# Wider products for up tiles 52 to 95 of an expert layer, and every fourth late tile's rest made by an adding DMA

## Chip, cores and metric

The kernel runs on one core of one Trainium2 chip. The metric is the device time of one launch in microseconds (us), the median of the runs shown; lower is better.

## What is computed

The reference is a stack of four blocks on 256 tokens of width 1024, in float32. The change touches only the expert layer ("PEER"), which stands in the first stack twice. Cut to what matters, and written as this kernel does it:

```
q      = h @ w_q                        8 heads, two halves of 128
scores = q_half @ sub_keys.T            top 16 of each half, then top 16 of the pairs
g      = softmax(top scores)            16 of 16384 experts, per head and token
up     = h @ peer_u.T                   256 x 16384: all experts, 128 tiles of 128
act    = gelu(up) * (sum of g at the chosen experts, else 0)
y      = act @ peer_v                   16384 x 1024: 128 down tiles
x      = x + gate * y
```

The kernel computes every expert for every token and weights the result, instead of gathering the chosen ones.

## The kernel before

Weights stream from HBM as tiles of 128 x 1024 float32 (512 KB) into a ring of four slots (`ring`, `RING = 4`). `refill` in the SyncE block issues the load of tile n+4 once tile n's slot is free, which is when `split_ready` counts tile n. All refills go through SyncE's one queue, in the order of `SEGMENTS`; beside them, at the start of `up0_late` and `up1_late` (the refill that tile 56 releases), SyncE runs `gate_row_out_sp`, which writes one row of 1024 values to HBM as 4-byte pieces (L784).

Products are float32 in three passes: each operand is split into a rounded high part and a rest, and high x high, high x rest and rest x high are summed. For the weights ACT makes the high part (`high`, L266, a rounding copy) and the DVE or POOL the rest (`rest`, L275, tile minus high), into one of four places of `wsplit`. `high(n)` waits for the tile and for PE to be done with tile n-4.

An up tile j gives 128 experts for all 256 tokens: eight chunks of the contraction. A narrow tile (`lin_cols`, `passes`, L240) takes three products of 256 columns per chunk, 24 in all. A wide tile (`wide_passes`, L246 and L247) takes two: the high part of the weights against the input's high part and rest side by side (512 columns, whole PSUM bank), and the rest against the high part (256 columns into the first half). Its two halves have to be added afterwards: ACT copies the second half out (L1567), the DVE adds the first (`summed`, L1706), and only then ACT takes the Gelu (L1570). Before the change tiles 30 to 50 are wide.

From tile 52 on the late phase runs: a routing step of four tokens stands behind seven of every eight tiles (`STEP_AT`, 64 steps). For step q the DVE builds one-hot matrices (`onehots`, L1741, `weighted_onehots`, L1747), PE multiplies them (`routing`, L1489), the DVE weights the tiles done so far for those tokens (`weigh`, L1714 and L1715), and ACT keeps the factors of later tiles in the places of their activations (`keep`, L1594). For a tile j in this phase the first `kept` tokens' Gelu stays in PSUM (L1574), the others go to the activations (L1576), and the DVE multiplies the kept ones by their factors (`weigh_tile`, L1723).

PE waits at the start of `up(j)` for `activated_ready` and `pr_weighted` of tile j-3, since three PSUM banks turn. The orders of ACT and DVE are written out by hand: ACT runs `keep` of tile j-1, `activate(j)` and in it `high` of tile j+3; the DVE's loop turn j runs the steps' work, the rest of tile j+2, the sum of tile j and the weighing of tile j-1. An instruction that waits holds everything behind it on its engine.

```python
for j in range(HEAD, 129):
    if j + 1 in STEP_AT: onehots(with_step(j + 1))
    if j - 1 in STEP_AT: weigh(with_step(j - 1))
    if j + 1 in STEP_AT: weighted_onehots(with_step(j + 1))
    if j + 2 < 131: up_rest(j + 2)
    if j < 128 and wide(j): summed(j)
    if j - 1 >= FIRST_STEP: weigh_tile(j - 1)
```

## Time and profile before

| | us |
|---|---|
| median of 3 runs | 2568.08 (2567.43 to 2568.27) |
| the profiled execution | 2567.51 |
| its span, first to last instruction | 2565.6 |
| PE busy | 2512.6 (98%) |
| DVE busy | 2037.3 (79%) |
| ACT busy | 1415.9 (55%) |
| POOL busy | 321.9 (13%) |
| granted TensorE clock | 0.994 of full speed |

The rows further down come from this one execution. Times are counted from its first instruction. A busy PE means that some product was in flight; the duration of one product contains its way through the array, so the pitch from one tile's start to the next is what a tile costs. "Idle before" names what ended an engine's wait.

### The profile page before, as it was taken

The page shows a single profiled execution, that of the slowest core. Times are in us where ns is not written, and L with a number is a line of the kernel's source. Part 1 is how long each engine was busy: PE and PEld are TensorE (multiplying, and loading weights), DVE is VectorE, ACT ScalarE, POOL GpSimd, SP SyncE. Part 2 cuts the span into 40 slices and gives each one's busy share as a digit, 9 for nine tenths or more (in the row PEclk, how much of TensorE's full clock was granted, in tenths as well). Part 3 has the DMA queues.
Part 4 walks back from the last instruction along what each step waited for, and adds up shares of the span by engine and source line. Part 5 has one row for each costly group of instructions (what it writes and reads, how often), then busy time and mean ns, then how long its engine had stood idle before and what let it go on. Part 6 is the DMA issues. An engine that isn't in the chain of part 4 may idle for free.

```text
span 2565.6 us, 46053 instructions
## 1 busy us (share of the span) xinstructions
PE 2512.6 (98%) x16116; PEld 2249.3 (88%) x16116; DVE 2037.3 (79%) x3624; ACT 1415.9 (55%) x2303; POOL 321.9 (13%) x182
## 2 busy tenths in 40 slices
PE   6999999999999999999999999999999999999998
PEld 5779989999888888889989999888888888889887
DVE  6778978899888887679888898666666886688766
ACT  3455575544565666555675545665554554464553
POOL 3107800000000002627500000000000001000000
PEclk9999999999999999999999999999999999999999
DMA  6844575444888885434664445555555355543554
GB/s 227 289 161 167 184 251 165 160 161 159 283 289 286 292 282 161 156 103 169 203 227 161 161 157 179 193 194 200 193 194 190 117 180 193 192 167 113 193 184 140
DMA packets 138422, 492.37 MB, mean 192 GB/s; under 512 B 18705, under 2 KB 18793, under 8 KB 137985
## 3 DMA queue, kind: packets, MB, share of 16 engines
q1 hardware_dynamic: 135600, 481.90, 55.3%
q0 software_dynamic: 2640, 8.02, 0.9%
q8 instruction: 118, 1.93, 0.3%
q14 instruction: 64, 0.52, 0.1%
HBM read 488.79 MB, written 1.07 MB: 191 GB/s over the span
## 4 chain that ended last, share of the span: by engine, by line
PE 87%; DVE 6%; DMA 3%; ACT 2%; issue 1%; POOL 0%; DVEq 0%; SPq 0%; ACTq 0%; POOLq 0%
PE ps L240 70%; PE ps L246 7%; PE ps L247 4%; PE ps L1489 2%; DMA weight_ring<-in_stream 2%; DVE weight_split L275 1%; ACT weight_split L266 1%; PE ps L2659 1%; PE ps L1453 1%; DVE hT_split L500 1%; DVE arena L742 0%; DVE hT_split L499 0%; DVE stat L625 0%; POOL weight_split L275 0%; PE ps L454 0%
## 5 line engine op out<-in xcount | busy, mean ns | idle before, releaser
L266 ACT ACTIVATE weight_split<-weight_ring 128x1024 fp32r<-128x1024 f32 x800 | 849.5, 1063 | 271.5 <-DMA weight_ring<-in_stream 181.6
L275 DVE TENSOR_TENSOR weight_split<-weight_ring,weight_split 128x1024 fp32r<-128x1024 f32 x684 | 830.4, 1222 | 163.7 <-ACT weight_split L266 161.6
L240 PE MATMUL ps<-hT_split,weight_split 128*128 128x256 f32 x7224 | 922.1, 286 | 3.9 <-POOL weight_split L275 1.5
L240 PE MATMUL ps<-weight_split,hidden_split 128*128 128x512 f32 x3948 | 911.6, 390 | 0.1
L240 PEld LDWEIGHTS ps<-hT_split,weight_split 128*128 128x128 f32 x7224 | 884.3, 192 | 10.3 <-issue 6.9
L240 PEld LDWEIGHTS ps<-weight_split,hidden_split 128*128 128x128 f32 x3948 | 735.9, 188 | 156.7 <-issue 1.4
L275 POOL TENSOR_TENSOR weight_split<-weight_ring,weight_split 128x1024 fp32r<-128x1024 f32 x116 | 282.7, 2443 | 122.2 <-ACT weight_split L266 122.0
L246 PE MATMUL ps<-hT_split,weight_split 128*128 128x512 f32 x816 | 291.4, 398 | 0.5 <-DVE hT_split L500 0.5
L1584 ACT ACTIVATE hidden_split<-arena 128x256 fp32r<-128x256 f32 (+1 forms) x256 | 173.9, 679 | 148.1 <-PE ps L240 148.0
L247 PE MATMUL ps<-hT_split,weight_split 128*128 128x256 f32 x816 | 229.0, 281 | 0.0
L1758 DVE TENSOR_TENSOR hidden_split<-arena,hidden_split 128x256 fp32r<-128x256 f32 x256 | 163.6, 639 | 81.6 <-ACT hidden_split L1584 81.6
L246 PEld LDWEIGHTS ps<-hT_split,weight_split 128*128 128x128 f32 x816 | 153.3, 188 | 37.5 <-DVE hT_split L500 1.1
L240 PE MATMUL ps<-weight_split,hT_split 128*128 128x512 f32 x660 | 158.7, 397 | 3.1 <-DVE weight_split L275 2.6
L247 PEld LDWEIGHTS ps<-hT_split,weight_split 128*128 128x128 f32 x816 | 154.0, 189 | 2.6
L1574 ACT ACTIVATE ps<-ps 128x256 f32<-128x256 f32 (+45 forms) x152 | 40.9, 269 | 208.0 <-PE ps L240 208.0
L240 PEld LDWEIGHTS ps<-weight_split,hT_split 128*128 128x128 f32 x660 | 123.7, 190 | 30.3 <-DVE weight_split L275 3.6
L1576 ACT ACTIVATE arena<-ps 128x256 f32<-128x256 f32 (+36 forms) x206 | 99.4, 483 | 75.5 <-PE ps L240 75.5
L742 DVE CUSTOM_DVE_ANT_0 arena<-weight_ring,silu_c_row 128x1024 f32<-128x1024 f32 x104 | 126.7, 1219 | 6.5 <-DMA weight_ring<-in_stream 5.5
L937 DVE TENSOR_TENSOR arena<-arena,ps 128x256 f32<-128x256 f32 x62 | 26.1, 421 | 106.7 <-ACT arena L897 106.7
L1741 DVE TENSOR_TENSOR step_places<-arena 128x1024 f16<-128x1024 f16 x128 | 88.3, 690 | 16.4 <-PE ps L1489 15.2
L1747 DVE TENSOR_TENSOR arena<-step_places,pick_parts 128x1024 f16<-128x1024 f16 x128 | 88.0, 688 | 0.7
L1832 POOL DMA_DIRECT2D arena<-in_sb_pairs x1 | 0.6, 644 | 677.8 <-DVE arena L556 677.8
(377 smaller groups left out, 1924.6 us busy)
## 6 DMA issues: line engine op xcount, KB each, us to landing
weight_ring<-in_stream SPq DMA_DIRECT2D x912, 512.0 KB, 4.2
arena<-gate_rows SPq DMA_DIRECT2D x3, 512.0 KB, 5.2
x<-in_x SPq DMA_DIRECT2D x1, 1024.0 KB, 5.1
arena<-mlstm_m_rows POOLq DMA_DIRECT2D x1, 1024.0 KB, 6.1
arena<-in_ln_mix_g POOLq DMA_DIRECT2D x2, 512.0 KB, 5.3
arena<-in_ln_mix_b POOLq DMA_DIRECT2D x2, 512.0 KB, 7.5
arena<-in_ln_ffn_g POOLq DMA_DIRECT2D x2, 512.0 KB, 4.6
arena<-in_ln_ffn_b POOLq DMA_DIRECT2D x2, 512.0 KB, 6.5
```

The costliest lines, as they stand in the source:

```text
L240: mm = pe.matmul(out_, stationary(s_part), moving(m_part), start=start and n == 0, stop=stop and n == 2, skip_group_check=True)
L246: pe.matmul(ps[:, bank, :].rearrange("p (k t) -> p k t", k=2), stationary(HIGH), moving, start=start, stop=stop, skip_group_check=True)
L247: return pe.matmul(ps[:, bank, 0:T], stationary(REST), moving[:, HIGH, :], start=False, stop=stop, skip_group_check=True)
L266: act.activation(wsplit[:, n % SPLITS, HIGH, :], ring[:, slot(POS[n]), :], ACT.Copy).then_inc(high_ready, 1)
L275: eng.tensor_tensor(w[:, REST, :], ring[:, slot(POS[n]), :], w[:, HIGH, :].bitcast(fp32), ALU.subtract).then_inc(split_ready, 1)
L742: dve.tensor_tensor_reduce(products, ring[:, slot(ADA_POS[a]), :], silu_row[:], 1.0, 0.0, ALU.mult, ALU.add, dots[:, row % 2, c:c + 1]).th ...
L1489: mm = pe.matmul(ps[:, q % 3, 128 * a:128 * a + 128], step_places[:, q % 2, 0, a, :], step_weights_in[:, q % 2, part, a, :], start=part == ...
L1576: step = act.activation(acts(j)[:, kept:T], bank[:, kept:T], ACT.Gelu)
L1584: act.activation(hidden[:, j % 3, HIGH, :], acts(j, i), ACT.Copy).then_inc(hidden_high, 1)
L1741: dve.tensor_tensor(step_places[:, q % 2].rearrange("p n a (j d) -> p (n a) j d", d=2), two_iotas, pr_places[:, q].rearrange("p n a d -> p ...
L1747: step = dve.tensor_tensor(step_weights_in[:, q % 2].rearrange("p k a (j d) -> p k a j d", d=2), step_places[:, q % 2, 1].rearrange("p a ( ...
L1758: dve.tensor_tensor(hidden[:, j % 3, REST, :], acts(j, i), hidden[:, j % 3, HIGH, :].bitcast(fp32), ALU.subtract).then_inc(hidden_ready, 1)
```

## The change

`WIDE` adds tiles 52 to 95 to the wide ones. In these the second half goes to a contiguous place, `second_halves`, and the sum goes back into PSUM, so that the Gelu has its two targets as in a narrow tile. The DVE's turn is reordered: the sum of tile j-1 and the weighing of tile j-2 stand in turn j.

`added(j)` is true for tiles 56, 60, ..., 124, 18 in a layer. For these ACT writes the negated, rounded tile into the rest's place right after the high part of tile j-1, POOL issues a DMA that adds the tile from the ring to it (512 KB, SBUF to SBUF), and the DVE, instead of making the rest, waits for that DMA in the turn of tile j-1 and counts the tile as split by a one-column memset. The high part of such a tile is made at once after the Gelu of tile j-4.

Besides, the `iota` table of 128 x 128 no longer has a place of its own: POOL loads it with the expert layer's parameters and the DVE casts it after the top-16 search; the first waits for constants are for 16 instead of 32; `EDGE` grows by 64 words, `step_weights_in` moves behind `second_halves`, and `halves_before` is `2 * len(WIDE)`. Cut of these lines, the diff is:

```diff
...
 FIRST_STEP = STEP_AT[0]
 EARLY = 51
 EXP_AT = 14
+WIDE = [j for j in range(128) if 30 <= j < 51 or 52 <= j < 96]
 def slot(pos):
...
         STEP = 4
         STEPS = T // STEP
         assert len(STEP_AT) == STEPS and EARLY < FIRST_STEP
-        step_weights_in = edge_b.bitcast(fp16).rearrange("p (r k a j) -> p r k a j", r=2, k=2, a=STEP)
+        second_halves = arena[:, ROUTE + 64 + 2 * T:ROUTE + 64 + 3 * T]
+        step_weights_in = arena[:, ROUTE + 64 + 3 * T:EDGE].bitcast(fp16).rearrange("p (r k a j) -> p r k a j", r=2, k=2, a=STEP)
         (pr_par, pr_q_out, pr_scored, pr_s_out, pr_topped, pr_chosen, pr_exp_in, pr_exp, pr_cols_t, pr_cols_out,
          pr_places_r, pr_parts_r, pr_built, pr_routed, pr_kept, pr_weighted) = (sem("peer_" + s) for s in (
              "params_in", "q_out", "scored", "scores_out", "topped", "chosen", "exp_in_ready", "exp_ready", "cols_turned", "cols_out",
...
         def weighted_count(l, j):
             return (128 - FIRST_STEP) * l + j - FIRST_STEP + 1
+        def added(j):
+            return FIRST_STEP + 4 <= j < 125 and j % 4 == 0
+
+        def added_count(l, j):
+            return sum(added(m) for m in range(128)) * l + sum(added(m) for m in range(j + 1))
+
         def wide(j):
-            return 30 <= j < 51
+            return j in WIDE
         def wide_count(l, j):
             return sum(wide(m) for m in range(128)) * l + sum(wide(m) for m in range(j + 1))
...
         def peer_pool(l):
             pool.wait_ge(src_ready, src_done(4 if l else 1))
             pool.dma_start(pr_sk, io["sub_keys"][l]).then_inc(pr_par, 16)
-            pool.dma_start(pr_iota16, io["iota"][:, 0:16]).then_inc(pr_par, 16)
+            pool.dma_start(pr_iota32, io["iota"]).then_inc(pr_par, 16)
             rests_pool(FIRST[f"peer{l}q"] + 3, 13)
             rests_pool(FIRST[f"up{l}"], HEAD)
+            for j in range(128):
+                if added(j):
+                    n, k = FIRST[f"up{l}"] + j, added_count(l, j)
+                    pool.wait_ge(negated, k)
+                    if k > 1:
+                        pool.wait_ge(added_in, 16 * (k - 1))
+                    pool.dma_start(wsplit[:, n % SPLITS, REST, :], ring[:, slot(POS[n]), :], accum_op=ALU.add).then_inc(added_in, 16)
         def peer_pe(l, turn):
             tq, tu, td = FIRST[f"peer{l}q"], FIRST[f"up{l}"], FIRST[f"down{l}"]
...
                 if s:
                     scores_out(s - 1)
+            def next_high(j):
+                if not added(j + 3):
+                    high(tu + j + 3)
+                if added(j + 4):
+                    n = tu + j + 4
+                    act.wait_ge(tile_full[slot(POS[n])], full(POS[n]))
+                    act.wait_ge(tiles_used, n - SPLITS + 1)
+                    act.activation(wsplit[:, n % SPLITS, REST, :], ring[:, slot(POS[n]), :], ACT.Copy, scale=-1.0).then_inc(negated, 1)
+
             def activate(j):
                 act.wait_ge(tiles_used, tu + j + 1)
-                if wide(j):
+                if wide(j) and j >= FIRST_STEP:
+                    act.activation(second_halves, second_of(4 + j % 3), ACT.Copy).then_inc(halves_copied, 1)
+                    next_high(j)
+                    act.wait_ge(halves_summed, wide_count(l, j))
+                elif wide(j):
                     act.activation(acts(j), second_of(4 + j % 3), ACT.Copy).then_inc(halves_copied, 1)
                     high(tu + j + 3)
                     act.wait_ge(halves_summed, wide_count(l, j))
...
                 if kept < T:
                     step = act.activation(acts(j)[:, kept:T], bank[:, kept:T], ACT.Gelu)
                 step.then_inc(activated_ready, 1)
-                high(tu + j + 3)
+                if not (wide(j) and j >= FIRST_STEP):
+                    next_high(j)
+                if added(j + 4):
+                    high(tu + j + 4)
             def hidden_top(j, i=0):
                 if not (isinstance(i, int) and j < 3):
...
             dve.tensor_tensor(g, e, pr_sum[:, 1].unsqueeze(2).broadcast_to([128, 16, 16]), ALU.mult).then_inc(pr_chosen, 1)
             def up_rest(j):
+                if added(j):
+                    return
+                if added(j - 1):
+                    dve.wait_ge(added_in, 16 * added_count(l, j - 1))
+                    dve.memset(stat[:, 252:253], 0.0).then_inc(split_ready, 1)
                 rest(dve, tu + j)
                 if HEAD <= j < HEAD + 16 and (j - HEAD) % 2:
                     ada_dve((104 if l else 40) + (j - HEAD) // 2, edge_b)
...
             def summed(j):
                 dve.wait_ge(halves_copied, wide_count(l, j))
-                dve.tensor_tensor(acts(j), acts(j), first_of(4 + j % 3), ALU.add).then_inc(halves_summed, 1)
+                first = first_of(4 + j % 3)
+                if j >= FIRST_STEP:
+                    dve.tensor_tensor(first, second_halves, first, ALU.add).then_inc(halves_summed, 1)
+                else:
+                    dve.tensor_tensor(acts(j), acts(j), first, ALU.add).then_inc(halves_summed, 1)
             def weigh(q):
...
                     onehots(with_step(j + 1))
                 if j - 1 in STEP_AT:
                     weigh(with_step(j - 1))
+                if j - 2 >= FIRST_STEP:
+                    weigh_tile(j - 2)
                 if j + 1 in STEP_AT:
                     weighted_onehots(with_step(j + 1))
+                if j - 1 >= FIRST_STEP and wide(j - 1):
+                    summed(j - 1)
                 if j >= 127:
                     down_rest(j - 127)
                 if j + 2 < 131:
                     up_rest(j + 2)
-                if j < 128 and wide(j):
+                if j < FIRST_STEP and wide(j):
                     summed(j)
-                if j - 1 >= FIRST_STEP:
-                    weigh_tile(j - 1)
+            weigh_tile(127)
             down_rest(2)
             dve.wait_ge(pr_weighted, weighted_count(l, 127))
```

In the changed file the lines have moved: L268 is `high`, L277 `rest`, L1586 the negated copy, L1592 the copy of a second half, L1603 and L1605 the Gelu, L1626 `keep`, L1735 the memset, L1745 `summed`, L1755 and L1756 `weigh`, L1764 `weigh_tile`, L1781 and L1787 the one-hots.

ACT before, from the keep of step 55 to that of step 58; `128x20` of L1574 is tile 56, and `tile_full0` is the ring slot of tile 60:

```order
L1594 ACTIVATE arena<-ps 128x4x73 [waits peer_done_tiles_weighted]
L1574 ACTIVATE ps<-ps 128x20 [waits tiles_used]
L1576 ACTIVATE arena<-ps 128x236
L266 ACTIVATE weight_split<-weight_ring 128x1024 [waits tiles_used,tile_full3]
L1594 ACTIVATE arena<-ps 128x4x72 [waits peer_done_tiles_weighted]
L1574 ACTIVATE ps<-ps 128x24 [waits tiles_used]
L1576 ACTIVATE arena<-ps 128x232
L266 ACTIVATE weight_split<-weight_ring 128x1024 [waits tiles_used,tile_full0]
L1594 ACTIVATE arena<-ps 128x4x71 [waits peer_done_tiles_weighted]
```

ACT now, the same place; `128x20` of L1603 is again tile 56:

```order
L1626 ACTIVATE arena<-ps 128x4x73 [waits peer_done_tiles_weighted]
L1592 ACTIVATE arena<-ps 128x256 [waits tiles_used]
L268 ACTIVATE weight_split<-weight_ring 128x1024 [waits tiles_used,tile_full3]
L1586 ACTIVATE weight_split<-weight_ring 128x1024 [waits tiles_used,tile_full0]
L1603 ACTIVATE ps<-ps 128x20 [waits wide_halves_summed]
L1605 ACTIVATE arena<-ps 128x236
L268 ACTIVATE weight_split<-weight_ring 128x1024 [waits tiles_used,tile_full0]
L1626 ACTIVATE arena<-ps 128x4x72 [waits peer_done_tiles_weighted]
L1592 ACTIVATE arena<-ps 128x256 [waits tiles_used]
L1603 ACTIVATE ps<-ps 128x24 [waits wide_halves_summed]
L1605 ACTIVATE arena<-ps 128x232
L1626 ACTIVATE arena<-ps 128x4x71 [waits peer_done_tiles_weighted]
```

The wait for `tile_full0` (tile 60) has moved from behind the Gelu of tile 57 to ahead of the Gelu of tile 56, with the negated copy (L1586), and the keep of step 56 (`128x4x72`) stands behind both.

DVE before, from the rest of tile 59 to that of tile 61; L1723 `128x20` weighs tile 56:

```order
L275 TENSOR_TENSOR weight_split<-weight_ring,weight_split 128x1024 [waits weight_high_ready]
L1723 TENSOR_TENSOR arena<-arena,ps 128x20 [waits peer_routing_kept,activated_ready]
L1714 TENSOR_TENSOR arena<-arena,ps 128x204 [waits activated_ready,peer_routing_built]
L1715 TENSOR_TENSOR arena<-arena,ps 128x4x6
L275 TENSOR_TENSOR weight_split<-weight_ring,weight_split 128x1024 [waits weight_high_ready]
L1723 TENSOR_TENSOR arena<-arena,ps 128x24 [waits peer_routing_kept,activated_ready]
L1741 TENSOR_TENSOR step_places<-arena 128x1024 [waits peer_routing_built]
L1714 TENSOR_TENSOR arena<-arena,ps 128x204 [waits activated_ready,peer_routing_built]
L1715 TENSOR_TENSOR arena<-arena,ps 128x4x7
L1747 TENSOR_TENSOR arena<-step_places,pick_parts 128x1024 [waits peer_onehots_ready]
L275 TENSOR_TENSOR weight_split<-weight_ring,weight_split 128x1024 [waits weight_high_ready]
```

DVE now, from the turn of tile 58 on; L1764 `128x20` weighs tile 56:

```order
L1755 TENSOR_TENSOR arena<-arena,ps 128x204 [waits activated_ready,peer_routing_built]
L1756 TENSOR_TENSOR arena<-arena,ps 128x4x6
L1764 TENSOR_TENSOR arena<-arena,ps 128x20 [waits peer_routing_kept,activated_ready]
L1745 TENSOR_TENSOR ps<-arena,ps 128x256 [waits second_halves_copied]
L1781 TENSOR_TENSOR step_places<-arena 128x1024 [waits peer_routing_built]
L1755 TENSOR_TENSOR arena<-arena,ps 128x204 [waits activated_ready,peer_routing_built]
L1756 TENSOR_TENSOR arena<-arena,ps 128x4x7
L1764 TENSOR_TENSOR arena<-arena,ps 128x24 [waits peer_routing_kept,activated_ready]
L1787 TENSOR_TENSOR arena<-step_places,pick_parts 128x1024 [waits peer_onehots_ready]
L1745 TENSOR_TENSOR ps<-arena,ps 128x256 [waits second_halves_copied]
L1735 MEMSET stat 128x1 [waits weight_added_in]
L277 TENSOR_TENSOR weight_split<-weight_ring,weight_split 128x1024 [waits weight_high_ready]
```

The rest of tile 60 is gone; in its place the memset waits for `weight_added_in`, with the rest of tile 61 queued behind it. The weighing of tile 56 stands a turn later, behind the weighing of step 57 (L1755, L1756), which waits for the Gelu of tile 56.

## Rows read from the trace of the kernel before

**Rows 1.** The page: TensorE's busy time, and the chain's shares by engine.

```profile
PE 2512.6 (98%) x16116; PEld 2249.3 (88%) x16116; DVE 2037.3 (79%) x3624; ACT 1415.9 (55%) x2303; POOL 321.9 (13%) x182
...
PE 87%; DVE 6%; DMA 3%; ACT 2%; issue 1%; POOL 0%; DVEq 0%; SPq 0%; ACTq 0%; POOLq 0%
```

**Rows 2.** Eight late up tiles each: length; PE, PEld, DVE, ACT, POOL busy; clock, DMA.

```profile
391.74:418.28 26.54, 26.54 (x251) 26.24 (x250) 21.86 (x45) 14.54 (x29) 0.00 (x0) 1.00 0.47 140
...
497.90:524.44 26.54, 26.54 (x251) 26.24 (x250) 24.08 (x45) 13.39 (x31) 0.00 (x0) 1.00 0.46 160
...
604.06:630.60 26.54, 26.54 (x251) 26.24 (x250) 26.11 (x45) 12.46 (x31) 0.00 (x0) 1.00 0.47 160
```

**Rows 3.** PE in order of time: start us, duration us, operation; wide, then narrow tiles.

```profile
332.24 0.48 PE L246 MATMUL ps<-hT_split,weight_split 128*128 128x512 f32 x1
...
388.86 5.92 PE L240 MATMUL ps<-hT_split,weight_split 128*128 128x256 f32 x48
394.62 0.62 PE L1489 MATMUL ps<-arena,step_places 128*128 128x128 f16 x8
```

**Rows 4.** SyncE in order of time, 400 to 403 us.

```profile
400.34 0.39 SPq L784 DMA_DIRECT2D gate_rows<-mods  x1
...
402.55 0.34 SPq L3025 DMA_DIRECT2D weight_ring<-in_stream  x1
```

**Rows 5.** The weight ring's tiles, 389 to 420 us: landing of its refills.

```profile
DMA to landing us min/median/max: 3.3/4.5/12.4
```

**Rows 6.** ACT, then DVE, in order of time; [idle before <-what ended it].

```profile
408.33 0.17 ACT L1574 ACTIVATE ps<-ps 128x20 f32<-128x20 f32 x1 [1.41 <-PE ps L240]
...
408.77 1.09 ACT L266 ACTIVATE weight_split<-weight_ring 128x1024 fp32r<-128x1024 f32 x1
409.88 0.41 ACT L1594 ACTIVATE arena<-ps 128x288 f32<-128x288 f32 x1
...
414.95 1.06 ACT L266 ACTIVATE weight_split<-weight_ring 128x1024 fp32r<-128x1024 f32 x1 [2.49 <-DMA weight_ring<-in_stream]
...
411.50 0.19 DVE L1723 TENSOR_TENSOR arena<-arena,ps 128x20 f32<-128x20 f32 x1
...
416.04 1.23 DVE L275 TENSOR_TENSOR weight_split<-weight_ring,weight_split 128x1024 fp32r<-128x1024 f32 x1 [3.41 <-ACT weight_split L266]
```

**Rows 7.** ACT in order of time, the same place in layer 1.

```profile
1358.87 1.06 ACT L266 ACTIVATE weight_split<-weight_ring 128x1024 fp32r<-128x1024 f32 x1 [2.34 <-DMA weight_ring<-in_stream]
```

**Rows 8.** PE in order of time, tiles 58 to 60 of layer 0.

```profile
411.95 3.11 PE L240 MATMUL ps<-hT_split,weight_split 128*128 128x256 f32 x24
...
415.33 5.99 PE L240 MATMUL ps<-hT_split,weight_split 128*128 128x256 f32 x48
```

**Rows 9.** Groups by line and shape, whole run: busy us, mean ns, idle before.

```profile
L897 ACT ACTIVATE arena<-ps 128x256 f32<-128x256 f32 x62 | 23.7, 382 | 102.5 <-PE ps L247 102.5
...
L1706 DVE TENSOR_TENSOR arena<-arena,ps 128x256 f32<-128x256 f32 x42 | 28.1, 669 | 21.1 <-ACT arena L1567 21.1
...
L937 DVE TENSOR_TENSOR arena<-arena,ps 128x256 f32<-128x256 f32 x62 | 26.1, 421 | 106.7 <-ACT arena L897 106.7
```

**Rows 10.** DMA issues 420 to 530 us: count, KB each, median us to landing.

```profile
weight_ring<-in_stream SPq DMA_DIRECT2D x34, 512.0 KB, 3.2
```

**Rows 11.** DMA issues of the whole run, one of POOL's.

```profile
arena<-in_hy_rope POOLq DMA_DIRECT2D x1, 512.0 KB, 3.5
```

**Rows 12.** Line L2530, POOL's 512 KB loads in pairs: issue to landing.

```profile
DMA to landing us min/median/max: 4.6/6.1/8.7
```

**Rows 13.** Stretches of 3.38 us: as rows 2, last the DMA share and GB/s.

```profile
413.42:416.80 3.38, 3.38 (x34) 3.34 (x33) 0.76 (x1) 1.85 (x4) 0.00 (x0) 1.00 1.01 390
416.80:420.18 3.38, 3.38 (x30) 3.38 (x29) 3.38 (x9) 2.69 (x6) 0.00 (x0) 1.00 0.80 288
```

**Rows 14.** DVE in order of time, the first microseconds.

```profile
7.97 0.76 DVE L732 TENSOR_SCALAR arena<-weight_ring,stat 128x1024 f32<-128x1024 f32 x1 [7.97 <-DMA iota<-in_iota]
9.50 2.68 DVE L735 SCALAR_TENSOR_TENSOR arena<-weight_ring,stat,arena 128x1024 f32<-128x1024 f32 x2 [0.78 <-DMA weight_ring<-in_stream]
```

More of the change, by code:

```diff
@@ L120, in build @@
         ident = sbuf("ident", [128, 128])
-        iota = sbuf("iota", [128, 128])
         stat = sbuf("stat", [128, 256])
@@ L230, in build @@
         out_done = sem("out_done")
+        negated = sem("weight_negated")
+        added_in = sem("weight_added_in")
         def passes(out_, stationary, moving, start, stop):
@@ L830, in split_wait @@
             pe.wait_ge(split_ready, i * (2 * PAIRS) + (n0 + p + 1))
-        halves_before = 42
+        halves_before = 2 * len(WIDE)
         def dense_pe(n0, n, jbefore, turn_n):
@@ L3074, in _ @@
         def _(eng):
-            eng.wait_ge(consts_in, 32)
+            eng.wait_ge(consts_in, 16)
             mlstm_pe()
@@ L3089, in _ @@
             eng.wait_ge(x_in, 16)
-            eng.wait_ge(consts_in, 32)
+            eng.wait_ge(consts_in, 16)
             mlstm_act()
@@ L3101, in _ @@
         def _(eng):
-            eng.wait_ge(consts_in, 32)
+            eng.wait_ge(consts_in, 16)
             eng.wait_ge(x_in, 16)
```

10 lines of the change are left out of this document (4 added, 6 removed).

## Prediction

> **What bounds the kernel now.** I read the page first. TensorE is busy for 98% of the span and its chain carries 87% of the end, so only what shortens or stalls TensorE counts [rows 1]. Next I cut the late up stretch of layer 0 into cycles of eight tiles (52 to 59, 60 to 67, ...). In each, PE is busy for all 26.54 us; the DVE takes 21.9 (first cycle) to 26.1 us (last) of it and ACT about half [rows 2]. So there is no PE idle time to win back, and the DVE has little room. Then come the PE rows at tile level. Two narrow tiles without a routing step take 394.62 - 388.86 = 5.76 us, 2.88 us each; a narrow tile with its routing step takes 3.38 us (411.95 to 415.33), so the step costs 0.50 us [rows 3, 8]. The twenty wide tiles 31 to 50 take 388.86 - 332.24 = 56.62 us, 2.83 us each [rows 3].
>
> One place in this stretch is not smooth. SyncE issues the 4-byte-wise write of `gate_rows` at 400.34 us, between the refills that tiles 55 and 56 release. The refill issued at 402.55 us (it brings tile 60) takes the 12.4 us to landing that are the longest there [rows 4, 5]. ACT sits idle 2.49 us and starts tile 60's high part at 414.95 us; the DVE's rest follows at 416.04 us [rows 6]. It ends at 417.27 us, and PE, which started tile 59 at 415.33 us, wants tile 60 at 415.33 + 2.88 = 418.21 us [rows 8]. This slow arrival is now hidden with 0.9 us to spare. Layer 1 does the same: there ACT idles 2.34 us until 1358.87 us [rows 7].
>
> **The change, part by part.**
>
> Wide products. A wide tile streams the same columns with 16 weight loads for 24. It saves 2.88 - 2.83 = 0.05 us, 44 tiles give 2.2 us in a layer and 4.4 us in both, all on PE. If the saving were nil next to routing steps this is 0; I see no row that would make it larger.
>
> Extra work on ACT and DVE. Each wide tile adds an ACT copy of 128x256 out of PSUM to a contiguous place (0.38 us by the L897 row) and a DVE add of PSUM and SBUF (0.42 us by L937; 0.67 us by L1706, which writes a strided place, is the upper end) [rows 9]. The new add reads and writes contiguous columns, so I take 0.42. In the cycle from 497.90 us (tiles 84 to 91) the DVE has 24.1 us; it gets 8 x 0.42 = 3.4, loses two rests of 1.2 us and gets two memsets of about 0.1: 25.2 us in a cycle that is then 26.15 us long [rows 2, 6, 9]. That fits, at 96%. Such an engine may fall behind within four tiles and catches up at the one without a rest. With 0.67 us per add it would be 27.2 us and would not fit. ACT has half its time free: the negated copies add 1.06 us each fourth tile and cost nothing by load.
>
> The rests by DMA. For tiles 56, 60, ..., 124 (18 in a layer) ACT writes the negated tile after tile m-4, POOL issues the adding DMA, and the DVE waits for it in its turn for tile m-1. Call A the time from issue to landing. No row shows an adding DMA. Nearest below: plain 512 KB refills, 3.2 us in this stretch; one 512 KB load issued by POOL, 3.5 us [rows 10, 11]. Nearest above: POOL's 512 KB loads in pairs beside the weight stream, 4.6 to 8.7 us [rows 12]. An add has to read the destination too, another 512 KB at the 288 to 390 GB/s that the engines moved when busy [rows 13], so 1.3 to 1.8 us more. I take 5.3 us in a quiet stretch, with 3.2 and 8.7 kept as ends.
> The Trainium skill ("Collectives: The Full Stack", section "The bandwidth ceiling: the fold count and why AG ≠ RS ≠ AR") says that a DMA that adds emits two read descriptors for each chunk and so runs at half a copy's rate. An estimate from that page and "DMA: Bandwidth & Descriptors" (2.0 us plus bytes over 436 GB/s) is 2.0 + 2 x 1.2 = 4.4 us; by it the steady stretch would be free of waits, as it is with my value.
>
> How long may A be? The ACT work after tile m-4 (2.83 us after its start) is copy 0.38, high part 1.06, negated copy 1.06: it is over 5.3 us after tile m-4 began. The DVE reaches the wait about 2.5 us into tile m-1, 3 x 3.33 + 2.5 = 12.5 us after the same point, and PE needs the tile at 13.3. That leaves 7.2 us; less 0.5 where one of the four tiles has no routing step and up to 1 us where ACT itself runs late behind the new add, 5.7. With A = 5.3 nothing is lost in the steady stretch.
>
> Tile 60. Here the change moves a wait. Before, ACT met tile 60's late landing after the Gelu of tile 57. Now the negated copy of 60 stands ahead of the Gelu of **56**, so everything of tile 56 waits for it. With the landing at 414.95 us, as before (the refill still stands behind the gate write; it is issued later, but was stuck anyway): negated copy 1.06, to 416.0; Gelu of 56, after which ACT is free 0.44 us later (408.33 to 408.77), at 416.45; high part of 60, 1.06, to 417.5; the keep of step 56, 0.4, to 417.9; the DVE's weighing of tile 56, 0.2, to 418.1 [rows 6]. PE's tile 59 waits for exactly that weighing: it starts 2.8 us late (415.33 before) and ends at 418.1 + 2.83 = 420.95 [rows 8]. Meanwhile the add, issued at 416.0, shares the engines with the refills of 61 to 63, which keep them at a share of 1.01 and 0.80 [rows 13]. I take A = 6.0 here: landing 422.0, memset, tile 60 at 422.1 us against 418.21: 3.9 us late. With A = 3.2 tile 59 decides and it is 2.7 us; with 8.7 us, 6.6.
> What the wide tiles 52 to 59 saved is lost in this wait; tiles 60 to 95 give back 36 x 0.05 = 1.8 us. Net per layer 3.9 - 1.8 = +2.1 us, both layers +4.2.
>
> Tile 56's own add is issued 2.5 us of ACT work after tile 52 ends at 394.6, near 397 us, ahead of the gate write, and has until 405 us: free. From 96 on the tiles are narrow, the DVE loses two rests a cycle and PE was full anyway: nothing. One weighing more stands at the end of the loop, 0.3 us for the DVE while PE has tiles 128 and on ahead: nothing.
>
> Start. The 64 KB table and its place in the first waits go: the DVE waited for it until 7.97 us, but at 9.50 us it already waits for the second weight tile [rows 14], so I take -0.2 us (bounds 0 and -1.5).
>
> **Sum:** +4.2 - 0.2 = +4.0 us. The profiled execution took 2567.51 us (span 2565.6), 0.57 under the median of the three runs; it would become 2571.5, and the median 2568.08 + 4.0 = 2572.1 us. A measurement of this kernel can tell 0.2%, 5.1 us, so the forecast lies just inside "no change". Its own range, from A at tile 60 (3.2 to 8.7 us), is +1.6 to +9.4: 2569.7 to 2577.5.
>
> **The rivals.**
> 1. *Faster, the wait doesn't appear.* If tile 60 lands by about 409 us (the gate write no longer in its way because the refill comes later, or done sooner), ACT doesn't block, and the full 4.4 us plus the start remain: 2563.5 us, down to 2562 with more from the start. For it: only the order of issue. Against it: the 12.4 us landing and the same delay in layer 1. It decides when tile 60 lands 5 us earlier.
> 2. *Slower, the adding DMA is too slow everywhere.* From A = 6.6 us on, about the middle of the 5.7 and 7.2 above, every one of the 36 adds holds PE by A - 6.6. A = 7.2 gives 36 x 0.6 = 22 us more: 2594; A = 6.9, 2583. For it: 4.6 to 8.7 us for POOL's loads in pairs [rows 12]. Against: those share the engines with another load issued 0.5 us apart.
> 3. *Slower, the DVE becomes the engine that sets the pace.* With an add of 0.67 us the DVE is over its cycle by 27.2 - 26.15 = 1.0 us; 5.5 cycles in two layers make 11 us: 2583. For it: 0.67 us is what the wide add costs today [rows 9]. Against: that one writes every 51st word of its place, the new one writes side by side.
> The Trainium skill ("SBUF — State Buffer", section "A bandwidth-pool intuition that's wrong (but worth ruling out)") warns that a DMA of GpSimd beside a DVE copy waits for its descriptors, 620 ns becoming 3100 ns. By that rule A would grow by up to 2.5 us and rival 2 would hold; here the DVE's work beside the adds is all two-input operations, which the same page, in "Who interferes with whom", takes to leave the writing of descriptors free.
> 4. *The wide tiles do not save.* Then 1.8 x 2 is not given back: 2575.7; it lies inside the ranges above.
>
> **How the numbers follow.** Forecast 0.60 (0.40 of it within 0.2%, 0.20 above, since A over 6.6 us at tile 60 crosses 5.1 us); rival 1, 0.11 (0.06 faster by over 0.2%, 0.05 within); rival 2, 0.20; rival 3, 0.09. That makes faster 0.06, same 0.45, slower 0.49. The range 2565 to 2592 leaves out the better half of rival 1 and the worse half of rival 2.
>
> **What would show it.** PE: wide tiles of 2.83 us from 52 to 95, a gap before tile 59 and one before tile 60, of 4 us together, in both layers, and no other in the stretch. ACT: idle before the negated copy of tile 60, ended by the weight ring's DMA, some 5 us long. The adds' time to landing: 4.5 to 6 us. DVE: 25 us of each cycle. Wrong would be: PE without a gap at 59 (rival 1), a gap before every fourth tile ended by the adding DMA (rival 2), or gaps growing towards tile 95 behind the DVE (rival 3).

## The result, and the profile after

| | before | after |
|---|---|---|
| median of 10 runs each, on one chip | 2568.03 us | 2573.33 us |
| lowest to highest | 2565.95 to 2570.48 | 2571.46 to 2576.70 |
| profiled execution (span) | 2567.51 (2565.6) us | 2572.41 (2570.6) us |

The ratio is 1.0022, with a 95% interval of 1.0015 to 1.0030: 5.3 us slower, just past the 0.2% that can be told from no change. The forecast was 2572.1 us.

The page's lines for all engines and for the chain, after:

```profile
PE 2510.1 (98%) x15412; PEld 2209.0 (86%) x15412; DVE 2024.8 (79%) x3712; ACT 1478.1 (58%) x2427; POOL 351.1 (14%) x217
...
PE 86%; DVE 6%; DMA 3%; ACT 2%; issue 2%; POOL 0%; SPq 0%; DVEq 0%; ACTq 0%
```

PE has 704 matmuls fewer (8 for each of 88 tiles), and "issue", time in which it waits for nothing that the profile shows, went from 1% to 2% of the chain [rows 1]. The cycles of eight late up tiles (length; PE, PEld, DVE, ACT, POOL busy; clock, DMA share, GB/s) tell where:

```profile
391.74:418.28 26.54, 24.42 (x179) 20.93 (x177) 20.63 (x42) 14.26 (x29) 0.94 (x2) 1.00 0.56 147
418.28:444.82 26.54, 24.74 (x163) 21.28 (x164) 22.69 (x53) 19.67 (x43) 2.56 (x3) 0.94 0.72 208
...
497.90:524.44 26.54, 26.54 (x189) 22.81 (x188) 24.13 (x54) 17.59 (x41) 1.74 (x2) 1.00 0.76 202
```

Before, PE was full in each [rows 2]. Now 3.9 us are missing around 418 us, in the cycle of tiles 52 to 59 and the next, and none later. In order of time (start, duration, instruction, idle before it), SyncE, ACT, the DVE and PE at that place:

```profile
401.61 1.09 SPq L786 DMA_DIRECT2D gate_rows<-mods  x1
...
416.91 1.06 ACT L1586 ACTIVATE weight_split<-weight_ring 128x1024 fp32r<-128x1024 f32 x1 [6.41 <-DMA weight_ring<-in_stream]
417.87 0.17 ACT L1603 ACTIVATE ps<-ps 128x20 f32<-128x20 f32 x1
...
...
418.64 0.37 DVE L1755 TENSOR_TENSOR arena<-arena,ps 128x204 f32<-128x204 f32 x1 [5.86 <-ACT arena L1605]
418.92 0.17 DVE L1756 TENSOR_TENSOR arena<-arena,ps 128x24 f32<-128x24 f32 x1
419.29 0.40 ACT L1626 ACTIVATE arena<-ps 128x288 f32<-128x288 f32 x1
419.79 0.19 DVE L1764 TENSOR_TENSOR arena<-arena,ps 128x20 f32<-128x20 f32 x1 [0.69 <-ACT arena L1626]
420.08 0.47 PE L248 MATMUL ps<-hT_split,weight_split 128*128 128x512 f32 x1 [3.92 <-issue]
```

ACT stands 6.41 us before the negated copy of tile 60 (L1586); the Gelu of tile 56 (L1603), the keep of its routing step (L1626) and the weighing (L1764) come behind it, and PE's tile 59 starts 3.92 us late. From the landing to that start it is 420.08 - 416.91 = 3.17 us. In layer 1 the same chain takes as long (1364.89 - 1361.72), and there tile 60 waits once more, for the memset that stands for its added rest:

```profile
1361.72 1.06 ACT L1586 ACTIVATE weight_split<-weight_ring 128x1024 fp32r<-128x1024 f32 x1 [2.81 <-DMA weight_ring<-in_stream]
...
1364.89 0.47 PE L248 MATMUL ps<-hT_split,weight_split 128*128 128x512 f32 x1 [2.88 <-issue]
...
1369.16 0.47 PE L248 MATMUL ps<-hT_split,weight_split 128*128 128x512 f32 x1 [1.25 <-DVE stat L1735]
```

In layer 0 tile 60 doesn't wait, because tile 59 itself ran slowly. PE's 512-column products of tile 59 (the last line is the second of tile 60), the memset that counts tile 60 as split, and the clock (third number from the end) of two stretches:

```profile
421.21 0.59 PE L248 MATMUL ps<-hT_split,weight_split 128*128 128x512 f32 x1
421.81 0.63 PE L248 MATMUL ps<-hT_split,weight_split 128*128 128x512 f32 x1
...
423.93 0.06 DVE L1735 MEMSET stat<- 128x1 f32 x1
...
424.86 0.40 PE L248 MATMUL ps<-hT_split,weight_split 128*128 128x512 f32 x1
```

```profile
421.00:423.00 2.00, 2.00 (x9) 1.66 (x8) 1.51 (x6) 1.81 (x6) 0.00 (x0) 0.56 0.90 176
423.00:425.00 2.00, 2.00 (x9) 1.77 (x8) 1.09 (x2) 1.06 (x4) 0.00 (x0) 0.58 0.02 2
```

After its 3.92 us of idleness, and 1.1 us of work, TensorE was granted about half its clock (1.2 for 2.4 GHz) for some 3.5 us. Six products and their partners took 424.86 - 421.21 = 3.65 us instead of 6 x 0.35: **1.5 us more, and no step of the forecast held a change of the clock.** Not all of it is new loss. At full clock tile 59 would have ended at about 420.08 + 2.83 = 422.91 us, and PE would then have waited for the memset, which ended at 423.99: 1.1 us. Tile 60 began at 424.37.

The pieces that I had to price without a row, after (issue to landing of the 36 adding DMAs; the DVE's sums, duration in ns: least, median, most; ACT's copies took 375/385/442):

```profile
DMA to landing us min/median/max: 5.1/5.4/7.4
```

```profile
L1745 DVE TENSOR_TENSOR ps<-arena,ps x88: 410/424/449, 399.3 to 1489.4; 128x256 f32<-128x256 f32 x88
```

For what follows I need a measure that leaves out the rest of the program: the late stretch, from the first to the last routing product of a layer (first and last start in the row of their line). Before it is 239.3 and 239.2 us; after:

```profile
L1505 PE MATMUL ps<-arena,step_places x512: 218/219/233, 395.6 to 637.9; 128*128 128x128 f16 x171
```

That is 242.3; layer 1, from 1341.5 to 1582.9 us, has 241.4. They are 3.0 and 2.2 us longer. In the program's early part, which is the same code in the change and in the first four experiments, these five profiled executions stand +1.2, +1.6, -2.0, -0.9 and +0.6 us from that of before at 170 us. So two us between profiled executions mean nothing, and what the removed table gave at the start (-0.2 us by the forecast) can't be resolved.

### The profile page after: what moved, and what is told of

It is laid out like the page before. It is cut to its first block, busy times and chain, and to the rows that moved or that the text cites. A ratio compares the mean times of both kernels' runs of the same rounds, so it can differ in the third digit from the quotient of the medians.

```text
span 2570.6 us, 44963 instructions
## 1 busy us (share of the span) xinstructions
PE 2510.1 (98%) x15412; PEld 2209.0 (86%) x15412; DVE 2024.8 (79%) x3712; ACT 1478.1 (58%) x2427; POOL 351.1 (14%) x217
## 4 chain that ended last, share of the span: by engine, by line
PE 86%; DVE 6%; DMA 3%; ACT 2%; issue 2%; POOL 0%; SPq 0%; DVEq 0%; ACTq 0%
PE ps L242 60%; PE ps L248 13%; PE ps L249 7%; DMA weight_ring<-in_stream 3%; PE ps L1505 2%; ACT weight_split L268 1%; DVE weight_split L277 1%; DVE hT_split L502 1%; PE ps L2702 1%; PE ps L1469 1%; DVE arena L744 1%; DVE hT_split L501 0%; DVE stat L627 0%; POOL weight_split L277 0%; DVE x L624 0%
## 5 line engine op out<-in xcount | busy, mean ns | idle before, releaser
L268 ACT ACTIVATE weight_split<-weight_ring 128x1024 fp32r<-128x1024 f32 x800 | 848.2, 1061 | 228.7 <-DMA weight_ring<-in_stream 133.5
L277 DVE TENSOR_TENSOR weight_split<-weight_ring,weight_split 128x1024 fp32r<-128x1024 f32 x648 | 786.4, 1223 | 139.4 <-ACT weight_split L268 132.6
L242 PE MATMUL ps<-hT_split,weight_split 128*128 128x256 f32 x5112 | 651.7, 286 | 4.7 <-POOL weight_split L277 2.0
L248 PE MATMUL ps<-hT_split,weight_split 128*128 128x512 f32 x1520 | 549.5, 403 | 8.5 <-issue 6.8
L249 PE MATMUL ps<-hT_split,weight_split 128*128 128x256 f32 x1520 | 426.7, 281 | 0.0
L277 POOL TENSOR_TENSOR weight_split<-weight_ring,weight_split 128x1024 fp32r<-128x1024 f32 x116 | 281.3, 2431 | 123.2 <-ACT weight_split L268 123.1
L1605 ACT ACTIVATE arena<-ps 128x256 f32<-128x256 f32 (+36 forms) x206 | 99.4, 482 | 75.4 <-PE ps L242 75.4
L1603 ACT ACTIVATE ps<-ps 128x256 f32<-128x256 f32 (+45 forms) x152 | 41.0, 270 | 152.2 <-DVE ps L1745 78.1
L1457 POOL DMA_DIRECT2D weight_split<-weight_ring x36 | 31.1, 862 | 585.0 <-ACT weight_split L1586 585.0
L1781 DVE TENSOR_TENSOR step_places<-arena 128x1024 f16<-128x1024 f16 x128 | 88.4, 691 | 22.6 <-PE ps L1505 21.9
L1787 DVE TENSOR_TENSOR arena<-step_places,pick_parts 128x1024 f16<-128x1024 f16 x128 | 87.8, 686 | 0.1
```

Of the source, the lines that this page charges most:

```text
L242: mm = pe.matmul(out_, stationary(s_part), moving(m_part), start=start and n == 0, stop=stop and n == 2, skip_group_check=True)
L248: pe.matmul(ps[:, bank, :].rearrange("p (k t) -> p k t", k=2), stationary(HIGH), moving, start=start, stop=stop, skip_group_check=True)
L249: return pe.matmul(ps[:, bank, 0:T], stationary(REST), moving[:, HIGH, :], start=False, stop=stop, skip_group_check=True)
L268: act.activation(wsplit[:, n % SPLITS, HIGH, :], ring[:, slot(POS[n]), :], ACT.Copy).then_inc(high_ready, 1)
L277: eng.tensor_tensor(w[:, REST, :], ring[:, slot(POS[n]), :], w[:, HIGH, :].bitcast(fp32), ALU.subtract).then_inc(split_ready, 1)
L1605: step = act.activation(acts(j)[:, kept:T], bank[:, kept:T], ACT.Gelu)
```

## The experiments

Theory: the late landing of tile 60, behind the write of the gate row in 4-byte pieces, now stops the Gelu of tile 56, and that alone turns the gain into a loss. Rivals: the adding DMA is too slow or too little ahead everywhere; the new order on the DVE costs time; the DVE is too full. Every kernel was timed beside the kernel before, and its ratio is against that.

### First four: where the wait goes, and what each half of the change does

**e1_from64**: adding DMAs only from tile 64 on.

```diff
-            return FIRST_STEP + 4 <= j < 125 and j % 4 == 0
+            return 64 <= j < 125 and j % 4 == 0
```

> The change with adding DMAs for tiles 64 to 124 only; tiles 56 and 60 get their rest from the DVE as before. Theory T (the time lost is the wait for tile 60's late landing, moved ahead of the Gelu of tile 56): PE's gaps of 4 us at tiles 59 and 60 in each layer shrink to under 1 us, the savings of 2.2 us a layer stay, 2564 to 2566 us, 7 to 9 us under the change's 2573.3. Rival S (the loss is spread over the late stretch, by the adding DMAs or by the DVE): two adds of 18 fewer, 2572 to 2573 us.

Measured: 2563.20 us against 2567.63, ratio 0.9982 (0.9973 to 0.9991). Two adding DMAs fewer in a layer are worth 9 to 10 us; I had expected 7 to 9. The stretches are 237.9 and 238.3. PE still waits once in each (0.99 and 1.4 us), since tile 60 lands late here too:

```profile
416.86 1.06 ACT L268 ACTIVATE weight_split<-weight_ring 128x1024 fp32r<-128x1024 f32 x1 [3.07 <-DMA weight_ring<-in_stream]
...
420.35 0.47 PE L248 MATMUL ps<-hT_split,weight_split 128*128 128x512 f32 x1 [0.99 <-DVE arena L1764]
```

**e2_gate32**: the whole change, the gate row written in 32-byte pieces (8 values of a partition together). The values lie in another order, so the gates that are read back later (of both expert layers and of one block between them) have their values in the wrong places.

```diff
-            sp.dma_start(gate_rows[(k - 1) * D:k * D].rearrange("(c p) -> p c", p=128), mods[:, row, :], ...
+            sp.dma_start(gate_rows[(k - 1) * D:k * D].rearrange("(p c) -> p c", p=128), mods[:, row, :], ...
```

> The change, but the gate row is written to HBM in pieces of 32 bytes instead of 4 (128 pieces instead of 1024), so its values land in another order: the later gates are therefore not the reference's. All adds as in the change. Theory T: the gate write no longer holds tile 60, which lands some 4 us after its refill; no gap at 59 and 60, 2564 us. If the late landing has another cause (the refill that waits for tile 56's add), ACT still waits before tile 60's negated copy and the time stays within 2 us of the change's 2573.3.

Measured: 2561.74 us, ratio 0.9974 (0.9963 to 0.9985). No wait is left; the first cycles are full, at full clock:

```profile
391.74:418.28 26.54, 26.54 (x191) 22.85 (x189) 23.92 (x54) 19.74 (x43) 1.80 (x2) 1.00 0.77 217
418.28:444.82 26.54, 26.54 (x189) 22.75 (x188) 23.00 (x54) 19.16 (x43) 1.70 (x2) 1.00 0.75 201
```

The stretches are 236.6 us both:

```profile
L1505 PE MATMUL ps<-arena,step_places x512: 219/219/233, 391.3 to 627.9; 128*128 128x128 f16 x171
```

So 44 wide tiles save 239.25 - 236.6 = 2.65 us, 0.06 each. The DMA engines around the write, 19 us of the change from 401 us in 40 slices (busy share in tenths, then GB/s):

```profile
DMA  9898997893200000336690105129167999699999
GB/s 241 164 267 164 216 259 259 294 135 113 11 0 0 0 0 0 43 86 34 43 34 17 26 9 43 26 26 69 9 112 276 414 414 345 267 371 388 397 397 354
...
weight_ring<-in_stream SPq DMA_DIRECT2D x5, 512.0 KB, 11.5
weight_split<-weight_ring POOLq DMA_DIRECT2D x1, 512.0 KB, 5.6
```

and the issues of e2_gate32 in 23 us from 397 us:

```profile
weight_ring<-in_stream SPq DMA_DIRECT2D x8, 512.0 KB, 4.1
weight_split<-weight_ring POOLq DMA_DIRECT2D x1, 512.0 KB, 5.6
gate_rows<-mods SPq DMA_DIRECT2D x1, 4.0 KB, 4.5
```

For 19 slices, some 9 us, the engines move 0 to 86 GB/s in the change, and the refills take 11.5 us; with 128 pieces for 1024 they take 4.1. The write in 4-byte pieces is the cause. How it holds the refills the records don't tell. Its pieces are recorded early in that time, up to about 406.3 us, and after them the engines are nearly idle. The packets of the change in the 2 us from 405 us and in the next 2:

```profile
DMA packets 747, 0.09 MB, mean 47 GB/s; under 512 B 725, under 2 KB 725, under 8 KB 747
```

```profile
DMA packets 4, 0.02 MB, mean 8 GB/s; under 512 B 0, under 2 KB 0, under 8 KB 4
```

**e3_adds**: the adding DMAs without the wide tiles.

```diff
-WIDE = [j for j in range(128) if 30 <= j < 51 or 52 <= j < 96]
+WIDE = list(range(30, 51))
```

> The change without the new wide tiles: tiles 52 to 95 are narrow again, the 18 adds a layer stay. Theory T: no saving of 4.4 us, and the wait at tile 60 stays, since the keep of step 56 still stands behind the negated copy and the high part: 2574 to 2577 us. If the wide tiles and their sums on the DVE were what costs (rival S), it would be at 2568 us.

Measured: 2576.29 us, ratio 1.0034 (1.0022 to 1.0046), as expected. The loss comes with the adding DMAs alone:

```profile
415.20 1.06 ACT L1586 ACTIVATE weight_split<-weight_ring 128x1024 fp32r<-128x1024 f32 x1 [7.45 <-DMA weight_ring<-in_stream]
...
417.90 1.41 PE L242 MATMUL ps<-hT_split,weight_split 128*128 128x256 f32 x5 [4.50 <-issue]
```

In the 2 us from 419 us the granted clock is 0.50 here as well. And it falls in layer 1 too, after a gap no longer than the one of the change that left it at full:

```profile
1367.18 5.02 PE L242 MATMUL ps<-hT_split,weight_split 128*128 128x256 f32 x27 [2.91 <-issue]
```

```profile
1367.00:1369.00 2.00, 1.82 (x8) 1.85 (x9) 1.75 (x6) 2.00 (x6) 0.00 (x0) 0.50 1.09 281
```

**e4_wide**: the wide tiles without adding DMAs; the DVE makes all the rests.

```diff
-            return FIRST_STEP + 4 <= j < 125 and j % 4 == 0
+            return False
```

> The change without adding DMAs: all rests by the DVE, tiles 52 to 95 wide. By my DVE ledger the sums put 27.5 us of work into cycles of 26.15 us from tile 60 on: some 3 to 4 us of waiting a layer against 2.2 us saved, 2569 to 2572 us, with PE's gaps behind the DVE's rest near the end of the wide tiles. If the DVE had room after all: 2564 us, and the adds were not needed.

Measured: 2563.37 us, ratio 0.9982 (0.9973 to 0.9991). **A miss**: I had the DVE over its cycle. It is nearly full, and PE still doesn't wait for a full DVE. It waits once in each layer (0.7 and 1.3 us), at the place of tile 60's late landing, and both waits are gone in e12_perm_wide below. Two cycles:

```profile
418.28:444.82 26.54, 26.54 (x188) 22.79 (x187) 26.41 (x57) 17.99 (x44) 0.00 (x0) 1.00 0.53 177
...
497.90:524.44 26.54, 26.54 (x189) 22.80 (x187) 26.20 (x54) 15.65 (x39) 0.00 (x0) 1.00 0.48 163
```

### Next four: whose queue, how much slack, and two controls

**e5_actgate**: the write still in 4-byte pieces, issued by ACT at tile 47 instead of by SyncE.

```diff
+                if j == 47:
+                    gate_row_out_act(3 if l else 1)
...
-            beside = {"up0_late": lambda: gate_row_out_sp(1), "down0_late": ...
-                      "up1_late": lambda: gate_row_out_sp(3), "down1_end": gate_peer1_sp}
+            beside = {"down0_late": ...
+                      "down1_end": gate_peer1_sp}
```

> The change whole, with the same small-piece gate row write, but issued by ACT at up tile 47 of each layer instead of by SyncE. If the PE wait behind tile 60 comes from SyncE's later weight loads standing behind this write in SyncE's own queue, then another queue frees them: no wait of ACT on the weight ring at tile 60, no PE gap after the first adding DMA, 2561 to 2564 us. If the small pieces slow the chip's DMA engines for every queue, the weight tile of step 60 still lands late and the time stays at 2571 to 2574.

Measured: 2565.14 us, ratio 0.9990 (0.9981 to 0.9999). Between the two outcomes that I had expected. In layer 0 PE waits 0.2 us in all (stretch 237.0); in layer 1 it waits 1.8 us for two added rests, 1.3 us the longer, and 0.6 us elsewhere (239.5). But the theory's own reason fell. The DMA queues and issues in 18 us from 380 us (packets, MB, share of the engines; KB each, us to landing):

```profile
q1 hardware_dynamic: 716, 2.61, 52.2%
q10 hardware_dynamic: 1040, 0.00, 2.9%
...
weight_ring<-in_stream SPq DMA_DIRECT2D x5, 512.0 KB, 8.9
gate_rows<-mods ACTq DMA_DIRECT2D x1, 4.0 KB, 9.6
```

The small packets are now in a queue of their own (q10), and SyncE's refills beside them still take 8.9 us, up to 12. So a write in another queue holds them as well, and standing behind it in SyncE's queue is not what it takes. Where they are held isn't shown: q10's packets took 2.9% of the engines' time. What helped was probably the time of the write: nine tiles earlier no negated copy of tile 60 waits behind it. That wasn't tried by itself.

**e6_delay**: e2_gate32, with eight memsets on POOL, each waited for, ahead of each adding DMA.

```diff
+                    for m in range(8):
+                        pool.memset(pad[:], 0.0).then_inc(padded, 1)
+                        pool.wait_ge(padded, 8 * (k - 1) + m + 1)
                     pool.dma_start(wsplit[:, n % SPLITS, REST, :], ring[:, slot(POS[n]), :], accum_op=ALU.add)...
```

> The kernel with the 32-byte gate pieces (2561.7 us), with 8 small memsets on POOL, each waited for, ahead of each of the 36 adding DMAs; they delay every rest by some 1 to 2 us. My slack for the steady stretch was 5.7 to 7.2 us against a landing of 5.3, threshold 6.6: past it each of the 36 adds would hold PE for what the delay exceeds the slack, so a delay of 1.5 us gives some 36 x 0.2 to 0.4 us, 2569 to 2576. If the routing steps left DVE and PE more slack than I reckoned, the time stays within 2 us of 2561.7.

Measured: 2613.60 us, ratio 1.0191 (1.0177 to 1.0205), 52 us over e2_gate32. **A miss**: I had expected 2569 to 2576. The delay (POOL's memsets, and the idle time ahead of the DMAs), the DMAs' landing, and two of PE's waits (in all, times, longest):

```profile
L1460 POOL MEMSET pad<- 128x64 f32 x288 | 43.8, 152 | 568.0 <-ACT weight_split L1591 553.6
L1462 POOL DMA_DIRECT2D weight_split<-weight_ring x36 | 31.1, 863 | 12.3 <-POOL pad L1460 12.3
```

```profile
DMA to landing us min/median/max: 5.3/6.2/8.0
```

```profile
PE ps L250 <- DVE stat L1740: 18.4, 17, 2.8
PE ps L244 <- DVE stat L1740: 17.2, 13, 2.7
```

The delay is (43.8 + 12.3) / 36 = 1.56 us; the landing itself takes 0.9 us longer than in e2_gate32 (5.3). Together each rest arrives about 2.4 us later, and PE waits 35.6 / 36 = 1.0 us for each; the stretches (264.3 and 258.2 us) grow by 1.4 us for each add, part of which is clock, 0.94 in one cycle that I looked at. So the steady stretch has 2.4 less 1.0 to 1.4, that is 1.0 to 1.4 us of slack. By this estimate, a mean over all adds, the threshold lies at 6.3 to 6.7 us from issue to landing, where I had put 6.6. What I had wrong here was the landing itself: delayed by 1.56 us, the adds also took 0.9 us longer, which I had put at nothing; past the threshold PE pays for that at nearly every add.

**e0_bgate32**: the kernel before with the 32-byte write (the same edit as e2_gate32, and the same effect on the gates).

> The kernel before, with the gate row written in 32-byte pieces alone. The value order of the later gates is another one. There the late weight tile met no instruction that needed it early, so the theory expects no change, 2566 to 2569 us. If the write cost PE time already in the kernel before, 2564 or less, and the change would then merely share that loss.

Measured: 2566.99 us against 2567.90, ratio 1.0002 (0.9992 to 1.0011). No change: before, the late landing was hidden.

**e7_order**: the change with the edits of both e3_adds and e4_wide, so that only the new order on the DVE stays.

```diff
+WIDE = list(range(30, 51))
...
+            return False
```

> The change's order on DVE and ACT alone: wide tiles only 30 to 50 as before, and no adding DMA. If the loss of the whole change came partly from that order, this is slower than before by 1 us or more; I expect 2567 to 2569, the kernel before's time, since no instruction is added or removed and every late rest still comes from DVE.

Measured: 2567.66 us, ratio 1.0001 (0.9992 to 1.0010). The order costs nothing that the time shows. It isn't without effect: in layer 1 PE waits 0.9 us once, near the late landing, where the kernel before doesn't wait (stretches 239.4 and 240.4).

### Last four: a version with the right output, and wide tiles to 124

**e11_perm**: e2_gate32, and the multiplications that use the gate read it as it lies; the output is the reference's. **e12_perm_wide**: that without adding DMAs. **e13_perm124**: e11_perm with wide tiles to 124. **e14_perm124_wide**: that without adding DMAs.

```diff
+                out, y, g = tok[:, tb, columns], y[:, columns], gate[:, columns]
+                if gate_k:
+                    out, y = (v.rearrange("q (c p) -> q c p", p=128) for v in (out, y))
+                    g = gate.rearrange("q (p c) -> q c p", c=8)[:, columns.start // 128:columns.stop // 128, :]
```

```diff
-WIDE = [j for j in range(128) if 30 <= j < 51 or 52 <= j < 96]
+WIDE = [j for j in range(128) if 30 <= j < 51 or 52 <= j < 125]
```

> The change whole with the gate row written in 32-byte pieces, and the six multiplications that use it reading the gate in the order in which it then lies, so that the output is the reference's. If the write's 4-byte pieces are the cause of the change's loss, 2560 to 2564 us, faster than before by over 0.2%, with no PE gap behind tile 60. If the strided reads of the gate cost DVE much, 2565 or more, with the six multiplications longer than before's.

> The same without adding DMAs: wide late tiles alone, every rest by DVE. The wide tiles alone took 2563.4 us with the 4-byte write, with PE gaps of 0.7 and 1.3 us behind it. If those gaps were the write's, this gives 2560 to 2563; if DVE's full queue costs the rest, it stays at 2563 to 2566 and the adding DMAs are worth 1 to 3 us.

> As e11_perm, with wide tiles up to 124 (29 more a layer). At 0.06 us a tile that e2_gate32 gave, 3.5 us less over both layers: 2557 to 2560. If the adding DMA's landing has too little slack once the pitch of a tile falls, or ACT's copy comes in the way of the last tiles, 2562 or more.

> As e13_perm124 without adding DMAs. DVE's windows are full with wide tiles at 52 to 95; the weigh operations grow with the tile's number, so if DVE sets the pace for tiles past 95, this is slower than e13_perm124 by 2 us or more; if DVE follows, the same within 1.5 us.

| | us | ratio (95%) | stretches |
|---|---|---|---|
| before | 2567.13 | | |
| e11_perm | 2563.28 | 0.9987 (0.9978 to 0.9996) | 236.6, 236.6 |
| e12_perm_wide | 2564.85 | 0.9994 (0.9985 to 1.0003) | 236.6, 236.7 |
| e13_perm124 | 2560.79 | 0.9977 (0.9968 to 0.9987) | 234.9, 236.1 |
| e14_perm124_wide | 2569.11 | 1.0009 (1.0000 to 1.0018) | 239.1, 239.0 |

e11_perm came as expected, though not over 0.2% faster than before. e13_perm124 is 0.8 us above its 2557 to 2560, and e14_perm124_wide is slower than it by over 2 us, which I had expected for a DVE that sets the pace. The strided reading costs e11_perm some of its gain. The gated products, before and in e11_perm (busy us, mean ns):

```profile
L562 DVE SCALAR_TENSOR_TENSOR arena<-ps,arena 128x512 f32<-128x512 f32 x16 | 11.0, 688 | 3.1 <-PE ps L240 3.0
```

```profile
L568 DVE SCALAR_TENSOR_TENSOR arena<-ps,arena 128x512 f32<-128x512 f32 x16 | 16.1, 1009 | 1.3 <-PE ps L242 1.3
```

With wide tiles to 95 the adding DMAs are worth nothing in the stretch (236.6 with and without), and neither kernel has a wait there; so the gaps of e4_wide were the write's. The 1.6 us between the two medians isn't placed. With wide tiles to 124 they are worth 8.3 us. The cycle from 603.6 us (tiles 116 on), e13_perm124 and then e14_perm124_wide:

```profile
603.60:630.00 26.40, 26.40 (x194) 22.95 (x193) 25.79 (x52) 15.49 (x42) 1.72 (x2) 1.00 0.73 214
```

```profile
603.60:630.00 26.40, 25.18 (x175) 20.82 (x173) 26.40 (x51) 12.98 (x35) 0.00 (x0) 1.00 0.43 146
```

Without them the DVE has no idle time left and PE starves. e13_perm124 is the fastest kernel here with the reference's output, 6.3 us under the kernel before. The 29 further wide tiles save 1.7 us in layer 0, as 29 x 0.06 does, and 0.5 in layer 1, where PE waits 0.9 us for an added rest.

## Why the prediction was right, and which of its steps were not

The time and its cause were right: 5.3 us slower by the medians where +4.0 was forecast, and both waits stand where they were placed in layer 1; in layer 0 the clock hid the second. The forecast put 0.40 of its 0.60 within 0.2% of before, and the result lies just past that. Step by step:

- **Wide products.** 0.05 us a tile forecast, 0.06 measured (e2_gate32), 2.65 us a layer for 2.2. The costs of ACT's copy (0.38; 0.385) and the DVE's sum (0.42; 0.424) were right, so rival 3 had no ground, and rival 4 fell with the first number.
- **The DVE's load.** 25.2 us forecast for the cycle from 497.90 us, 24.1 measured. The error shows in e4_wide: without the adding DMAs I reckoned more than a cycle holds, and all of it fitted. The sum added whole durations to a busy time; instructions that follow each other closely overlap (L1755 above ends at 419.01 us, L1756 begins at 418.92), and a busy time counts an overlap once. For eight sums that is some 0.7 us of the 1.1, and the memsets lie inside the rest beside them. In e4_wide it explains about half of the error (27.5 reckoned, 26.2 to 26.4 measured); the other half is open.
- **The adding DMA.** 5.3 us forecast, 5.4 measured; 5.6 at tile 60, where I had 6.0. The estimate of 4.4 us that I had worked out from the Trainium skill ("Collectives: The Full Stack", section "The bandwidth ceiling: the fold count and why AG ≠ RS ≠ AR", and "DMA: Bandwidth & Descriptors", section "Anatomy of one DMA — SWDGE (gpsimd) path") is a microsecond short. Its warning of a GpSimd DMA held beside DVE work ("SBUF — State Buffer", section "A bandwidth-pool intuition that's wrong (but worth ruling out)") didn't come true: no add took over 7.4 us. Rival 2 fell, though not by much: e6_delay puts the threshold about a microsecond above the landing.
- **Tile 60.** The chain from the landing to PE's tile 59 was forecast at 418.1 - 414.95 = 3.15 us and took 3.17. The landing was 416.91 us, not 414.95 "as before". Of these 2.0 us, 0.8 is where the execution itself stood (PE was ready for tile 59 at 420.08 - 3.92 = 416.16 us, against 415.33). The other 1.1 is the step that failed. I had let the refill come later at no cost, since it was stuck behind the write anyway. Tile 56 is now counted by the memset, a DVE turn later than by the rest before, so its refill was issued 3.8 us after the write (405.40 and 401.61 us) and not 2.2 (402.55 and 400.34 [rows 4]); it landed 15.3 us after the write's issue, not 14.6. That is 0.7 us; the other 0.4 is that PE, with wide tiles behind it, was ready that much sooner against the write. Hence 3.92 us for 2.8. In layer 1 the gap was 2.88, near the forecast.
- **The second wait.** 1.1 us forecast before tile 60; 1.25 in layer 1. In layer 0 the clock took its place, at 1.5 us. **The clock was missing from the sum**; by the working above it cost some 0.4 us over the wait that it replaced. In e3_adds it fell in both layers.
- **What held the refill.** I wrote of a refill standing behind the gate write. e5_actgate shows that a write in ACT's queue holds SyncE's refills as well, so it is something that both queues share; which part isn't shown.

These idle times are a little short of what was lost, because idle time counts from the end of the last product, and in a full stretch the next one starts before that end. In layer 1 tile 59 starts 3.50 us after the routing products begin (1361.39 to 1364.89 us), where the next tile with such products in front needs 0.43 (1372.01 to 1372.44): 3.07 us lost for 2.88 of idle time. In the same way it is 1.42 for 1.25 at tile 60, and 4.11 for 3.92 in layer 0. So layer 0 gives 4.11 + 1.5 - 2.65 = +3.0 us (measured 3.0), layer 1 gives 3.07 + 1.42 - 2.65 = +1.8 (measured 2.2; 0.4 us there isn't placed).

The forecast had 4.3 us of waiting in each layer (3.9 late at tile 60, and the 0.4 that tiles 52 to 59 save), where the stretches have 5.7 and 4.8 more than those of e2_gate32 (242.3 and 241.4 less 236.6): 1.9 us too little over both. It had 2.2 us of saving in each for 2.65: 0.9 us too little. The two errors have opposite effects, and that the sum came so near is in part luck. Rival 1, the refill out of the write's way, is what e2_gate32 made by hand: 2561.7 us, where 2563.5 had been worked out.

## What to carry to other kernels

Where an instruction that waits for a transfer is moved ahead of others on an engine that works in order, look for the one place where that transfer is late and hidden: every instruction behind it inherits the wait, and a stall of 3 to 5 us can cost TensorE its clock afterwards, as three of the four here did. A small transfer can be the most expensive one: beside 4 KB in 4-byte pieces the 512 KB loads took 9 to 12 us to land instead of about 4, in another queue too. Before work is taken off an engine, measure once with the work left there: here the relief was worth nothing with 44 wide tiles a layer, and 8 us with 73.

## What the hardware showed that I had not expected

- A 4 KB write in 1024 pieces on ACT's queue (2.9% of the engines' time by its packets) raised SyncE's 512 KB refills from about 4 us to 8.9 to 12 us. The Trainium skill ("DMA: Bandwidth & Descriptors", section "Why small descriptors are slow (HBM only)") gives a fixed cost per packet, but nothing on neighbours; what holds them is not shown by these runs, and the engines' own records are nearly empty while the loads wait (4 packets in the 2 us from 407 us).
- After 3.92 us without work the granted clock stayed at full for about 1.1 us of products and was then near half for some 3.5 us. After gaps of 0.99, 1.4 and 2.88 us it stayed at full. In e3_adds, after gaps of 4.50 and 2.91 us, it was at 0.50 from the first microsecond of products on. So two gaps of nearly the same length, 2.88 and 2.91 us, ended differently, and the gap's length alone doesn't decide it.
- A DVE product of 128x512 that reads one input at a stride of eight values took, over 16 of which 12 are such, 5.1 us more: about 0.43 us each on top of 0.69.
